# Long MLP of an encoder layer in two phases, its up projection by seven half-depth products

## What is computed

```python
x = layer_norm(ALPHA * x + mix, ln1_g, ln1_b)
hu = depthwise_conv(x @ w_up + b_up, w_ffn_conv, b_ffn_conv, FFN_CONV_PAD)
val, gt = jnp.split(hu, 2, axis=-1)
ffn = (jax.nn.gelu(gt) * val) @ w_down + b_down
return layer_norm(ALPHA * x + ffn, ln2_g, ln2_b)
```

## Time and profile before

| what | us |
|---|---|
| runs of the kernel, three | 2744.11, 2746.22, 2748.4 |
| their median | 2746.22 |
| profiled execution: first to last instruction (span) | 2743.4 |
| PE busy in it | 2659.9 |
| DVE, ACT, POOL busy | 1486.2, 768.5, 653.2 |

### The profile page before, as it was taken

One profiled execution on the slowest core, in us unless ns is written; L12 is line 12 of the kernel. 1 busy time (PEld: TensorE's weight loads), 2 busy tenths in 40 slices (PEclk: granted clock), 3 DMA queues, 4 the chain that ended last, 5 costly groups with the idle time before them and its releaser, 6 DMA issues.

```text
span 2743.4 us, 32010 instructions
## 1 busy us (share of the span) xinstructions
PE 2659.9 (97%) x11898; PEld 2193.1 (80%) x11898; DVE 1486.2 (54%) x1780; ACT 768.5 (28%) x1053; POOL 653.2 (24%) x332
## 2 busy tenths in 40 slices
PE   8998999999999999999999999989999999999998
PEld 6786888888788877888888888878788778888886
DVE  6799754334504568644545464667742414644445
ACT  3565713313400022010101111148932301211112
POOL 3554532232133622434243332310000000000000
PEclk9999999999999999999999999999999999999999
DMA  6554554444596823435343433456656693544554
GB/s 216 198 196 157 200 184 157 173 161 168 201 375 230 314 87 129 157 133 180 129 181 124 177 129 147 148 210 219 227 199 229 218 355 134 207 184 187 198 199 166
DMA packets 168544, 519.94 MB, mean 190 GB/s; under 512 B 13255, under 2 KB 40135, under 8 KB 166384
## 3 DMA queue, kind: packets, MB, share of 16 engines
q1 hardware_dynamic: 113536, 422.02, 42.6%
q10 hardware_dynamic: 54896, 96.39, 9.9%
HBM read 303.13 MB, written 206.32 MB: 186 GB/s over the span
## 4 chain that ended last, share of the span: by engine, by line
PE 83%; DVE 10%; DMA 3%; ACT 3%; issue 1%; SPq 0%; ACTq 0%; DVEq 0%
PE ps L877 49%; PE ps L1218 12%; PE ps L1045 8%; PE ps L1139 4%; PE ps L927 3%; PE ps L1028 2%; PE ps L1078 1%; DMA gate_in<-gate_dram 1%; DMA W<-w_split 1%; PE ps L1065 1%; PE ps L930 1%; PE ps L1207 1%; DVE tau L1801 1%; DVE tau L1791 0%; DVE acc L2082 0%
## 5 line engine op out<-in xcount | busy, mean ns | idle before, releaser
L877 PE MATMUL ps<-XH,W 128*128 128x512 f32 x4224 | 1206.0, 391 | 26.9 <-DVE XL L1746 11.7
L877 PEld LDWEIGHTS ps<-XH,W 128*128 128x128 f32 x4224 | 794.8, 188 | 203.9 <-issue 19.6
L877 PE MATMUL ps<-XL,W 128*128 128x512 f32 x2112 | 710.0, 390 | 0.0
L877 PEld LDWEIGHTS ps<-XL,W 128*128 128x128 f32 x2112 | 397.9, 188 | 82.4
L1218 PE MATMUL ps<-W,HH 128*128 128x512 f32 x1152 | 310.1, 389 | 1.5 <-DVE HL L2065 1.5
L1218 PEld LDWEIGHTS ps<-W,HH 128*128 128x128 f32 x1152 | 216.1, 188 | 46.8 <-DVE HL L2065 1.9
L761 POOL TENSOR_SCALAR W<-raw 128x1024 fp32r<-128x1024 f32 (+2 forms) x72 | 91.4, 1270 | 566.8 <-PE ps L877 301.7
L1045 PE MATMUL ps<-XH,W 128*128 128x512 f32 x672 | 216.4, 393 | 0.0
L827 POOL TENSOR_SCALAR W<-raw 128x1024 fp32r<-128x1024 f32 x72 | 86.8, 1205 | 536.8 <-PE ps L877 228.8
L762 POOL TENSOR_TENSOR W<-raw,W 128x1024 fp32r<-128x1024 f32 (+2 forms) x72 | 205.6, 2855 | 6.0
L828 POOL TENSOR_TENSOR W<-raw,W 128x1024 fp32r<-128x1024 f32 x72 | 190.3, 2643 | 6.0
(11 more groups left out here) (205 smaller groups left out, 3341.8 us busy)
## 6 DMA issues: line engine op xcount, KB each, us to landing
w_split<-W SPq DMA_DIRECT2D x131, 1024.0 KB, 6.2
W<-w_split SPq DMA_DIRECT2D x130, 1024.0 KB, 6.8
raw<-w_mlp SPq DMA_DIRECT2D x72, 512.0 KB, 4.2
raw<-w_qkv_mix SPq DMA_DIRECT2D x28, 512.0 KB, 3.7
w_split<-W SPq DMA_DIRECT2D x8, 1280.0 KB, 12.3
W<-w_split SPq DMA_DIRECT2D x8, 1280.0 KB, 8.3
gate_dram<-mix_out ACTq DMA_DIRECT2D x16, 512.0 KB, 2.7
gate_in<-gate_dram ACTq DMA_DIRECT2D x16, 512.0 KB, 6.2
```

Of the source, the lines that this page charges most:

```text
L877: last = nc.tensor.matmul(bank(group, c), lhs(wl, k), rhs(xl, k, c), start=(k == 0 and n == 0), stop=(k == nk - 1 and n == 2))
```

## The change

It concerns the MLP alone. The names of its code are after those of Strassen's method, in the form with seven products and shared sums.

**Up, long sequence.** x1 is cut by feature halves and token halves, the weights of a pair by feature halves and gate against value. Two pairs (PLAIN) are still done as before. The other 22 (FAST) take seven products of half the depth (4 tiles of features, 512 tokens: 12 matmuls each) in place of eight. The products need four other forms of x, T1 to T4, made once (sums on DVE and POOL, 128x2048 each; heads on ACT, tails on DVE and POOL), and per pair four sums S1 to S4 of weight blocks and the blocks A11, A12, A22: four TENSOR_TENSOR of 128x512 on POOL for the sums, seven heads on ACT, seven tails on POOL (`pair_forms`). Two sets of forms alternate; a set is free again when PE has done all seven products of two pairs before. Three banks of PSUM per pair are filled twice or three times; ACT evicts the first product (`l_e`, first_product) and the gate's first half, DVE adds the others out of PSUM (`gate_second`, `value_second`, `second_halves`, `value_first`) between the taps of the pair before (`pair_period`). The gate's middle tap goes to ACT (`centre`). h (`l_h`, unsplit) goes to DRAM.

**Down, long sequence.** It starts after all of up. All 24 hidden tiles are summed in PSUM, first for token tiles 0 to 3 (eight banks), then for 4 to 7: 48 steps of 24 matmuls, with the down weights loaded and split by POOL in both halves, and h loaded back (256 KB a step) and split by DVE (`split_down_h`). The last three steps of a half finish tile by tile. The first layer norm's rows go to DRAM and come back into `acc_down`.

**Short sequence.** Nothing of the MLP is saved in `w_split`. SP loads the 72 MLP slabs anew (512 KB each), and POOL splits each (`split_short`), in the same slots with the same waits for their last users.

```diff
+PLAIN = 2
+FAST = FT - PLAIN
+PE_ORDER = ("A11", "S2", "S1", "A12", "S3", "S4", "A22")
+DONE_ORDER = ("A11", "A12", "A22", "S2", "S1", "S3", "S4")
+ADDED_ORDER = ("S1", "S2", "S3", "S4")
+FORM_BANKS = ((0, 1, 2), (4, 5, 6))
+STEPS = 2 * FT
+RING = 4
+LAST_K = 3
...
+        def wait_pair_slots(eng, j):
...
+            else:
+                eng.wait_ge(form_used, 7 * j - 7)
...
+                    def pair_forms(j, side, between=lambda: None):
+
+                        F = forms[side]
+                        low = {n: form_sum[side][n][:, :] for n in ADDED_ORDER}
...
+                        wait_pair_slots(pool, j)
+                        pool.tensor_tensor(low["S1"], weight_raw("A21"), weight_raw("A22"), ALU.add).then_inc(form_added, 1)
...
+                        for i, n in enumerate(DONE_ORDER):
+                            pool.wait_ge(form_rounded, 7 * j + i + 1)
+                            src = weight_raw(n) if n[0] == "A" else low[n]
+                            pool.tensor_tensor(F[n][:, 1, :], src, F[n][:, 0, :].bitcast(F32), ALU.subtract).then_inc(form_done, 1)
+                            pool.wait_ge(form_done, 7 * j + i + 1)
...
+                def split_short(g, n, free):
...
+                    pool.wait_ge(slab_done, free)
...
+                            pe.wait_ge(form_done, 7 * j + 1)
+                            form_product(a, "A11", "B11", True, side)
...
+                            pe.wait_ge(form_done, 7 * j + 4)
+                            form_product(b, "S2", "T2", True, side)
+                            pe.wait_ge(form_done, 7 * j + 5)
+                            form_product(c, "S1", "T1", True, side)
+
+                            pe.wait_ge(form_evac, 2 * j + 1)
+                            form_product(a, "A12", "B21", False, side)
...
+                            pe.wait_ge(form_taken, 5 * j + 1)
+                            form_product(b, "S3", "T3", False, side)
...
+                        def pair_period(j, side, ahead=True):
+                            first_product(j, side)
+                            if ahead:
+                                round_plain_forms(j + 1, 1 - side)
+                            gelu(j + PLAIN - 1)
+                            if ahead:
+                                round_sums(j + 1, 1 - side)
+                            gate_half(j, side)
+                            centre(j + PLAIN)
...
+                    def pair_period(j, side):
+
+                        p = j + PLAIN - 1
+                        gate_taps(p, lambda: value_first(j - 1, 1 - side))
+                        value_taps(p, lambda: gate_second(j, side))
+                        value_second(j, side)
+                        hidden(p)
+                        second_halves(j, side)
```

More of the change, by code:

```diff
@@ new lines, in next_pair, with load_down, load_h @@
+                def next_pair(j):
+                    sp.wait_ge(form_done, 7 * j - 4)
+                    load_pair(j + PLAIN)
+                    store_h(j - 1)
+                next_pair(1)
+                with sp.Fori(0, FAST // 2 - 1) as i:
+                    for k in range(2):
+                        next_pair(2 * i + 2 + k)
+                def load_down(s, kk, k):
+                    sp.dma_start(raw[k][:, 0:D_MODEL], A["w_down"][kk, :, :]).then_inc(raw_in[k], 16)
+                def load_h(kk, half, slot):
+                    sp.dma_start(H_down[slot][:, 1, :].bitcast(F32), h_dram[kk, :, half * CH:(half + 1) * CH]).then_inc(h_landed[slot], 16)
@@ L691, in _ @@
+                for slot in range(4):
                     sp.wait_ge(w_saved[slot], 16 * TOTAL[0][slot])
@@ L848, in _ @@
+                    for s in range(RING):
+                        down_slab(s, s // 2, s)
+                    with order.loop(STEPS // RING - 1, RING) as i:
+                        for k in range(RING):
+                            down_slab(RING * i + RING + k, 2 * i + 2 + k // 2, k)
                 q, T = 1, SEQS[1]
@@ L1625, in take_back @@
                     def take_back(half):
+                        kept = q == 0 and half
+                        if kept:
+                            act.wait_ge(z_stored[0][0], 16 * (KD // 2 + 4))
                         for k in range(KD):
@@ L1628, in take_back @@
                             act.wait_ge(back[q], g + 1)
[L1629 removed]
+                            if g >= 2 and not kept:
                                 act.wait_ge(x1_split[q], g - 1)
[L1631 removed]
+                            A1(x1b[:, k, :] if kept else x1[g % 2][:, 0:TH], ps[:, 4 + 2 * half + k % 2, 0:TH], ACT.Identity, scale=col("ln1_g", k),
                                bias=col("ln1_b", k)).then_inc(x1_made[q], 1)
@@ L1689, in _ @@
                     if q == 0:
-                        for slot in range(2, 5):
+                        for slot in range(2, 4):
                             act.wait_ge(w_saved[slot], 16 * TOTAL[0][slot])
@@ new lines, in hidden, with gap, value_first @@
+                    def hidden(p):
+                        dve.wait_ge(gelu_done[0], p + 1)
+                        if not (isinstance(p, int) and p == 0):
+                            dve.wait_ge(h_stored, 16 * p)
+                        tell(V.tensor_tensor(l_h[:, :], lv_conv[:, :], lg_conv[:, :], ALU.mult), h_ready, p + 1)
+                    def gap(j):
+                        return small[:, bass.ds(160 + PLAIN + j, 1)]
+                    def value_first(j, side):
+                        dve.wait_ge(form_used, 7 * j + 7)
+                        tell(V.scalar_tensor_tensor(out=lv_raw[:, 1:CH + 1], in0=ps[:, FORM_BANKS[side][1], :], scalar=gap(j),
+                                                    in1=l_e[side][:, :], op0=ALU.add, op1=ALU.add), form_taken, 5 * j + 5)
@@ new lines, in _ @@
+                    if q == 0:
+                        long_up()
+                        long_sum()
+                    else:
+                        pair(0, 0)
+                        dve.wait_ge(rows_in[q], 48)
+                        order(V.scalar_tensor_tensor(out=down_row[:, :], in0=b1_row[:, :], scalar=ALPHA, in1=down_row[:, :],
+                                                     op0=ALU.mult, op1=ALU.add))
+                        for tt in range(nt // 2):
+                            start_sum(tt)
+                        pair(0, 1)
+                        for tt in range(nt // 2, nt):
+                            start_sum(tt)
+                        pair(0, 2)
+                        pair(0, 3)
+                        for tt in range(nt):
+                            add_down(0, tt)
+                        with order.loop(NG - 2, FG * 6) as i:
+                            for n in range(FG):
+                                pair(i + 1, n)
+                            for tt in range(nt):
+                                add_down(i + 1, tt)
+                        for n in range(FG):
+                            pair(NG - 1, n)
```

705 lines of the change are left out of this document (565 added, 140 removed).

## The result

The changed kernel takes 2795.37 us (median of three runs, 2794.97 to 2797.58) against 2746.22: **slower, ratio 1.0182, 95% interval 1.0163 to 1.02**. The prediction was 2740 with a range up to 2775, so the result lies outside it. The span of the profiled execution is 2795.8 us against 2743.4, so 52.4 us are to be found; the forecast had -6.

A forecast was written before the change was run, and what follows sets the result against it. The prediction took TensorE, busy 97% of the span, as the bound. Up -35, down +7, between the sequences -5 and short MLP +27 gave -6: 2746.2 to 2740 us, own range 2722 to 2760, with rivals 2700 to 2775.

The forecast's parts named there:

- down in two halves: Long down: steps hidden by TensorE except at the start (+3) and the turn of the halves (+4); +7 us, 0 to +15.
- the short MLP: Short sequence: GpSimd's slab splits, in turns with VectorE, make TensorE wait for HL; +27 us, 0 to +50.
- fewer matmuls: Up: 22 of 24 pairs take 7 products of 12 matmuls instead of 96 matmuls; -59.9 us.
- the pace set by GpSimd: Up: GpSimd's pair lasts 20.2 us against TensorE's 19.04, over 21 pairs; +24.4 us, bounds 0 to +56.
- The sign that I had named for it: Up: TensorE should wait for GpSimd's low parts before S2; no size given.
- The turn of the sequences: Between the long down and the second sequence: VectorE is done about 4 us sooner; -5 us, 0 to -8.
- The wait at the start of down: Start of down: VectorE's first h split and the last value_first stand behind GpSimd's turns; +3 us.
- the half boundary: Turn of down's halves: VectorE has a last sum, two output rows and two splits while GpSimd bursts three slabs; +4 us.
- The filling: Start of up: forms and T4 come late, so the form pairs start 5 us behind; +5 us, 0 to +15.
- the eight x1b buffers: Start of up: separate buffers end the wait of 3.27 us at 1036.74; -3 us.
- the short MLP stalls in every group: Rival, chance 0.18: the fourth down slab waits for h, 10 us instead of 2 in four groups; 2772 us.
- clock in the up phase: Rival, chance 0.07: repeated short TensorE waits lower the clock, costing 2 us in each of 21 pairs; 2782 us.

The follow-up runs named there:

- e7: Changed kernel with down mended (six of eight z1 sums), plus ScalarE making each form pair's first value tap in up instead of VectorE: 2769.59 us.
- e9: Changed kernel with down mended, ScalarE making short-MLP slab heads, and VectorE instead of GpSimd making A22's low part in up: 2722.56 us, ratio 0.9918.
- e11: e9 with GpSimd's sum for T3 held back until VectorE has split all of x: 2725.53 us, ratio 0.9927.
- e2: Changed kernel with SP waiting for the last h store to land only before loading tile 22: 2786.69 us, ratio 1.016.
- e3: Changed kernel with ScalarE's z1 loads issued one tile per step and the short sequence's x after step 10: 2792.12 us, ratio 1.0173.
- e4: Changed kernel with VectorE's z1 sums one per two steps and two h splits ahead of the output rows at the half boundary: 2781.10 us, ratio 1.0137.
- e6: Changed kernel with down mended (six of eight z1 sums), plus ScalarE making short-MLP slab heads from the sixth on instead of GpSimd: 2742.47 us, ratio 0.9989.

## Why the prediction was wrong

**The step that failed.** Two terms of the sum were far too small, down in two halves (+7, measured +37.3) and the short MLP (+27, measured +52.5), and of the 58.4 us that I was off they hold 55.8. In down the mechanism itself was wrong: I called the steps "hidden by TensorE", and there TensorE waited for a load behind a store and for VectorE's sums. In the short MLP the mechanism was right and its size was not.

**What held.** -59.9 for fewer matmuls, less the pace set by GpSimd: 20.04 us per pair where I had 20.2, and GpSimd 91% busy where I had asked for 80% or more. The sign that I had named for it did not show: TensorE's waits are for VectorE's sum ahead of the product with T4, not for low parts ahead of S2. That GpSimd's list sets the pace is shown by e7 and e9, not by who ended those waits. The turn of the sequences: -5.6 for -5. The wait at the start of down, 3.02 us for +3, and the places of the waits at the half boundary and in the short MLP.

**The filling and the eight x1b buffers** (+5 and -3): together +9.8 in place of +2. By the measured period, up would be -59.9 + 21 x 1.0 - 1.5 = -40.4; it is -30.6. The x1b buffers ended ScalarE's wait, but I had not asked what GpSimd does at that moment: its T3 sum is the longest instruction of the phase, and VectorE's cast met it. e11 shows that this wait was not the bound either.

**Down in two halves** (+7, bounds 0 to +15): +37.3. This was the worst step. I had costed the start and the half boundary and called the rest "hidden by TensorE", by mean loads per step. Two places were missing: SP's wait for the last store ahead of the loads (9.63 us, e2 and e3: store and loads among 6 MB that ScalarE issues at once), and VectorE's sums on z1, for which my sum had no term at all; I had noted only that the eight adds per group "fall away" (4.82 us, e4). At the half boundary the mechanism was as predicted and the size off: 2.40 and 6.66 us, with the clock at 0.56 and 0.60 behind them, for +4. The waits are 26.7 of the 37.3 us; the other 10.6 are matmuls at the lower clock behind them, for which I had taken nothing.

**The short MLP** (+27): +52.5. The mechanism is the predicted one, as e6 shows: VectorE in turns with GpSimd. The sizes: from the turn-back to the first eviction of g +10.3 for +4 (2358.08 - 2322.09 = 36.0 us in place of 2347.90 - 2322.21 = 25.7; the clock fell there too, to 0.83 from 2320 to 2340); group 0 waited 12.3 us (from its first eviction of g to the first add 66.4 us in place of 50.6, so +15.8) for +11; groups 1 to 4 waited 2.92, 2.63, 2.63 and 2.64 for 2 each, but each also lost about as much to the clock, so from group 1 to group 2 it takes 2563.03 - 2491.70 = 71.3 us where the earlier trace rows had 66.1 (2464.65 - 2398.51): +5.2 and not +2. The last group's wait of 5.64 us for HL stands against my +5 and 1.5. What I had as a rival, "the short MLP stalls in every group", with 10 us a group and the clock falling after waits of over 3 us, came true at half its price and below its own threshold.

**The clock.** I had let only waits of 3 us and more cost clock. In the windows behind the waits of 2.92 and 2.63 it was at or near the lower level (1.2 GHz):

```profile
2491.00:2495.00 4.00, 3.30 (x8) 2.63 (x9) 0.91 (x2) 0.00 (x0) 0.03 (x1) 0.50 0.40 131
...
2562.00:2566.00 4.00, 2.97 (x7) 2.40 (x8) 0.91 (x2) 0.00 (x0) 0.36 (x1) 0.55 0.41 131
```

The rival "clock in the up phase" did not come: waits of 0.7 us in every pair left it at 1.00 throughout.

The sum of the misses: +4.4 (up), +30.3 (down), -0.6, -1.2, +25.5 (short MLP) are the 58.4 us between -6 and +52.4. Just over half of them is in down, which I had worked out in one short paragraph.
